# A gather row of 32 tokens by four expert slots in place of 128 tokens by one, and another order of the first gathers, sorts and projections

## The chip, the cores and the metric

The kernel runs on one core of a Trainium2 chip. The metric is device time in microseconds (us) of one execution: the median of three runs. The engines named are TensorE (PE), VectorE (DVE), ScalarE (ACT), GpSimd (POOL) and SyncE (SP). All arithmetic that matters here is float32.

## The reference

The input is 512 tokens of width 1024, with 16 learned "meta" tokens in front. There are two layers. The first has a mixer of attention and a short convolution, the second one of window means; both are followed by the same kind of expert layer, which makes nearly all of the time:

```python
def one_block(hb):                                   # tokens after rms_norm
    q = (hb @ w_query).reshape(t, 8, 2, 128)
    s = einsum('thpc,phkc->thpk', q, keys)           # 128 keys in each of two lists
    sv, si = lax.top_k(s, 16)                        # per list
    cand     = sv[:, :, 0, :, None] + sv[:, :, 1, None, :]
    cand_idx = si[:, :, 0, :, None] * 128 + si[:, :, 1, None, :]
    top_s, top_pos = lax.top_k(cand, 16)             # of 256 pairs
    idx  = take_along_axis(cand_idx, top_pos)        # (t, 8 heads x 16) experts
    gate = softmax(top_s)
    act  = gelu(einsum('tnd,td->tn', expert_u[idx], hb))
    return einsum('tn,tnd->td', gate * act, expert_v[idx])
h = h + one_block(rms_norm(h))
```

So each token has 128 slots: in each slot it fetches one of 16384 experts, a vector u for a dot with the token's `hb` and a vector v for a weighted sum. Kept together they are 8 KB.

## The kernel before

**Tiles and rows.** The 16 meta tokens are one job, the 512 others four tiles of 128 tokens, and there are two layers: after the meta tokens (they are needed in the first layer only) come the kernel's tiles 0 to 7, of which 0 to 3 are layer one. The unit of the stream is the *row*: one indirect gather of 128 partitions of 8 KB. For a tile, a row is one slot of all 128 tokens, so a tile has 128 rows; for the meta tokens, a row is 16 tokens by eight slots, so they have 16. In all there are 16 + 8 x 128 = 1040 rows. Sixteen rows are a *chunk*, four a *quad*.

**What a row does.** POOL issues the gather (line 1437) into a ring of six groups, each of 3 x 1024 floats a partition, so that u of one row lies over v of the row before. DVE multiplies u with `hb`, held in PSUM (`hd`), and sums along the width: a *dot* (line 1617). After each quad DVE starts the gelu (`gelu_argument`), ACT takes one exponential (line 1549), DVE makes four weights of it (`gelu_weights`, line 1599), and ACT writes, one row after the other, a matrix `w_col` with the weights on its diagonal (line 1559). PE multiplies it with v and adds into the open sum `y_ps` in PSUM: two matmuls of 128x512 a row (line 1496). For the meta rows `w_col` is 128x16, and four matmuls of 256 columns go to four groups of 32 PSUM partitions (line 1464). A gather into a ring group waits for the dot of the row before in that group and for the sum of the row before that (`Place`): with all six groups in use for the dot of row n-6 and the sum of row n-12.

**The order.** Each engine runs its own instructions in order; other engines are waited for by semaphores. The four functions of the last part write down that order by hand: `tile(j, hooks)` walks through the 128 rows of a tile, and a hook (row, step) puts another step behind that row. In this way the routing of the next-but-one tile (its queries on PE, eight steps of two matmuls each for one *piece* of two heads; the sort on DVE in thirteen stages, `topk_stages`) runs between the rows of tile j. Tiles 6 and 7 route nothing more.

**The beginning.** The mixer leaves `catT`, which PE multiplies with the output matrix: the *out-projection* (`project_tensor`, a half of 512 columns each call, numbered 2 to 9; 2 and 3 are tile 0, 4 to 9 tiles 1 to 3). Half 4 and later ones are taken to SBUF by ACT (`take_projected`). Two of the six ring groups, `ring_late`, lie where operands of these projections are, so they can be used only when all are done. The first eight gathers therefore go to the four early groups, and then POOL waits in `late_constants` for the last projection, before it clears `prev` and goes on:

```python
META_ORDER = [0, 1, 2, 3, 0, 1, 2, 3, 4, 5, 0, 1, 2, 3, 4, 5]
            gather_pool(pool, None, 0, range(EARLY_ROWS))          # eight
            late_constants(pool)
            gather_pool(pool, None, 0, range(EARLY_ROWS, CHUNK))
```

The meta tokens are routed first, all eight heads in one sort; PE then picks the 128 indices for each row out of the result with small matmuls (`meta_select_tensor`, line 1129), ACT stages them, and the first gather goes. Tile 0's first two pieces are queried and sorted in that time too (`first_query`), its other two between rows.

## Time and profile before

| what | value |
|---|---|
| median of 3 runs | 3069.64 us (3068.76 to 3072.61) |
| the profiled execution: its own time | 3071.45 us |
| its span, first to last instruction | 3069.7 us |
| first gather issued at | 337.81 us |
| PE busy | 85% of the span (line 1496: 4096 records, 1986 us) |
| DVE busy | 68% |
| POOL busy | 32% |
| ACT busy | 19% |
| mean granted clock of PE | 0.943 of full speed |
| moved by DMA | 1139 MB, 371 GB/s over the span |

How to read the rows: a time line starts with when it begins and how long it took, then engine, line of the kernel, operation, what it writes `<-` what it reads, shapes (partitions x elements), and how many instructions were put together in it; behind it, in brackets, is how long the engine stood idle before, and what it then waited for. A float32 matmul stands in these rows as two records, so "x16" is eight matmuls. `PEclk` is the clock that PE was granted, as a share of full speed. Lines of a window give for each engine its busy time and its instructions, then that clock, the share of time that the DMA engines were busy, and GB/s. Times of the rows count from the first instruction of the span.

### The profile page before, as it was taken

To read this page: it belongs to the slowest core of one execution; us is meant where nothing else is said; L and a number is where in the kernel's file an instruction comes from. 1 tells how busy PE (TensorE), PEld (TensorE's weight loads), DVE (VectorE), ACT (ScalarE), POOL (GpSimd) and SP (SyncE) were. 2 spreads that over 40 slices of the span, in tenths; PEclk is the share of its full clock that TensorE was granted. 3 is DMA by queue.
4 is the path that set the end of the run, shared out by engine and by line. 5 is a ranking of instruction groups with operands and counts; after the bars stand their busy time and mean duration, and the time that the engine had idled before them with its cause. 6 is when DMAs were issued, how large, how long until landed. Compare 5 with 4: busy or idle time off the path is not lost.

```text
span 3069.7 us, 27540 instructions
## 1 busy us (share of the span) xinstructions
PE 2618.8 (85%) x7006; PEld 1210.0 (39%) x7006; DVE 2096.7 (68%) x6440; ACT 582.0 (19%) x1769; POOL 997.0 (32%) x1107
## 2 busy tenths in 40 slices
PE   9999869897988789778988889888988889877777
PEld 4765424343443334333434334343434334333323
DVE  2143568887778668666788677866877688755555
ACT  2035112111111111112111211121112111111111
POOL 0000033333443333333333333333333333333332
PEclk9999989999999999889999999999998999999899
DMA  5131289999999999999999999999999999999998
GB/s 190 60 130 55 110 330 413 391 395 421 421 421 410 403 421 413 421 414 416 415 408 418 414 407 419 410 414 421 404 410 414 412 416 409 415 408 422 421 421 331
DMA packets 165560, 1139.24 MB, mean 371 GB/s; under 512 B 18672, under 2 KB 19696, under 8 KB 29984
## 3 DMA queue, kind: packets, MB, share of 16 engines
q0 software_dynamic: 149760, 1090.59, 86.6%
q1 hardware_dynamic: 15648, 46.94, 4.0%
q8 instruction: 57, 0.93, 0.1%
q14 instruction: 95, 0.78, 0.1%
HBM read 1135.30 MB, written 2.10 MB: 371 GB/s over the span
## 4 chain that ended last, share of the span: by engine, by line
DMA 50%; PE 33%; DVE 11%; issue 6%; ACT 1%; POOLq 0%; POOL 0%; SPq 0%; DVEq 0%
DMA ring_early<-in_peer_uv,idx_u 17%; DMA ring_early<-in_peer_vu,idx_u 17%; PE psum L1496 16%; DMA ring_late<-in_peer_uv,idx_u 9%; DMA ring_late<-in_peer_vu,idx_u 6%; PE psum L1071 5%; DVE ring_early L1617 4%; PE psum L713 3%; PE psum L755 2%; PE psum L616 2%; DVE ring_late L1617 2%; PE psum L649 1%; DVE work L1188 1%; DVE si L1186 1%; PE psum L578 1%
## 5 line engine op out<-in xcount | busy, mean ns | idle before, releaser
L1496 PE MATMUL psum<-ring_early,w_col 128*128 128x512 f32 x2736 | 1321.4, 626 | 252.3 <-ACT w_col L1559 238.8
L1617 DVE SCALAR_TENSOR_TENSOR ring_early<-ring_early,psum 128x1024 f32<-128x1024 f32 x696 | 846.9, 1217 | 413.5 <-DMA ring_early<-in_peer_uv,idx_u 209.7
L1496 PEld LDWEIGHTS psum<-ring_early,w_col 128*128 128x128 f32 x2736 | 537.3, 201 | 955.5 <-issue 789.5
L1496 PE MATMUL psum<-ring_late,w_col 128*128 128x512 f32 x1360 | 664.9, 628 | 123.3 <-ACT w_col L1559 113.6
L1617 DVE SCALAR_TENSOR_TENSOR ring_late<-ring_late,psum 128x1024 f32<-128x1024 f32 x344 | 418.6, 1217 | 222.9 <-DMA ring_late<-in_peer_uv,idx_u 144.7
L1437 POOL DMA_INDIRECT ring_early<-in_peer_vu,idx_u x348 | 329.2, 946 | 598.2 <-DVE ring_early L1617 285.9
L1437 POOL DMA_INDIRECT ring_early<-in_peer_uv,idx_u x348 | 326.8, 939 | 585.3 <-DVE ring_early L1617 307.7
L1559 ACT ACTIVATE w_col<-ident,weight 128x128 f32<-128x128 f32 x1024 | 343.9, 392 | 644.9 <-DVE weight L1599 638.3
L1496 PEld LDWEIGHTS psum<-ring_late,w_col 128*128 128x128 f32 x1360 | 267.3, 201 | 471.5 <-issue 407.9
L1549 ACT ACTIVATE ge<-ga 128x4 f32<-128x4 f32 (+1 forms) x265 | 54.3, 205 | 1359.7 <-DVE ga L1585 1359.7
L1071 PE MATMUL psum<-wq,hbT 128*128 128x512 f32 x512 | 274.5, 623 | 23.9 <-DVE work L1188 22.8
L1437 POOL DMA_INDIRECT ring_late<-in_peer_uv,idx_u x172 | 162.2, 943 | 293.9 <-DVE ring_late L1617 175.6
L1437 POOL DMA_INDIRECT ring_late<-in_peer_vu,idx_u x172 | 161.6, 940 | 269.5 <-PE psum L1496 116.5
L1071 PEld LDWEIGHTS psum<-wq,hbT 128*128 128x128 f32 x512 | 101.8, 201 | 157.6 <-issue 129.7
L505 POOL IOTA iota<- 128x16 f32 x1 | 0.1, 144 | 283.6 <-ACT catT L848 283.6
L713 PE MATMUL psum<-hT,w_ring 128*128 128x264 f32 x384 | 86.2, 387 | 1.7 <-ACT qkv L799 1.7
L713 PEld LDWEIGHTS psum<-hT,w_ring 128*128 128x128 f32 x384 | 72.7, 190 | 15.1 <-ACT qkv L799 2.0
L1593 DVE TENSOR_SCALAR ge<-ge 128x4 f32<-128x4 f32 (+1 forms) x265 | 44.2, 167 | 23.9 <-ACT ge L1549 23.9
L755 PE MATMUL psum<-w_ring,catT 128*128 128x512 f32 x128 | 57.2, 601 | 0.0
L1617 DVE DVE_READ_ACCUMULATOR ring_early<-ring_early,psum 128x1 f32 x696 | 57.1, 82 | 0.0
L616 PE MATMUL psum<-w_ring,hT 128*128 128x512 f32 x128 | 55.5, 594 | 0.0
L1595 DVE RECIPROCAL ge<-ge 128x4 f32<-128x4 f32 (+1 forms) x265 | 47.0, 177 | 9.1
(237 smaller groups left out, 1728.9 us busy)
## 6 DMA issues: line engine op xcount, KB each, us to landing
wq<-in_peer_w_query SPq DMA_DIRECT2D x16, 1024.0 KB, 18.0
w_ring<-in_even_w_in SPq DMA_DIRECT2D x5, 2048.0 KB, 8.1
ring_early<-in_peer_vu,idx_u POOLq DMA_INDIRECT x348, 12.9
ring_early<-in_peer_uv,idx_u POOLq DMA_INDIRECT x348, 12.9
w_ring<-in_even_w_out SPq DMA_DIRECT2D x1, 4096.0 KB, 13.9
ring_late<-in_peer_vu,idx_u POOLq DMA_INDIRECT x172, 12.9
ring_late<-in_peer_uv,idx_u POOLq DMA_INDIRECT x172, 12.9
hT<-in_x_T SPq DMA_DIRECT2D x4, 528.0 KB, 7.4
```

What stands on the lines that cost most here:

```text
L578: last = nc.tensor.matmul(psum[:, 4 + t, :], hT[:, k, block_of(t)], w_ring[:, 0, k, :], start=(k == 0), stop=(k == KD - 1))
L616: last = nc.tensor.matmul(psum[0:n, 4 + i % 4, :], hT[:, k, block_of(t)], w_ring[:, g % 2, k, :], start=(k == 0), stop=(k == KD - 1))
L713: last = nc.tensor.matmul(psum[:, 4 + 2 * (i % 2) + half, 0:HALF], w, hT[:, k, HALF * half:HALF * half + HALF], start=(k == 0), stop=(k == ...
L755: last = nc.tensor.matmul(dst, catT[:, k, cols_of(t)], w_out_sb[:, k, c], start=(i < 4 and k == 0), stop=(k == KD - 1))
L1071: ins = nc.tensor.matmul(dst[0:n, :], hbT[:, k, 0:n], wq[:, k, bass.ts(s, 512)], start=(k == 0), stop=(k == KD - 1))
L1437: nc.gpsimd.indirect_dma_start(pair_cells(at), None, uv_rows if at.side else vu_rows, bass.IndirectOffsetOnAxis(idx_u[par][:, i:i + 1], 0) ...
L1496: ins = nc.tensor.matmul(y_ps[:, half, :], w_col[:, i % W_SLOTS, :], v_cell(at)[:, 512 * half:512 * half + 512], start=False, stop=stop, s ...
L1549: nc.scalar.activation(ge[:, 0:n], ga[:, 0:n], ACT.Exp, scale=-GELU_B).then_inc(s_gexp, 1)
L1559: nc.scalar.activation(w_col[:, i % W_SLOTS, 0:cols], base[:, 0:cols], ACT.Copy, scale=weight[par][:, i:i + 1]).then_inc(s_wcol, 1)
L1593: c.did(nc.vector.tensor_scalar(ge[:, 0:n], ge[:, 0:n], 1.0, None, ALU.add))
L1595: c.did(nc.vector.reciprocal(ge[:, 0:n], ge[:, 0:n]))
L1617: nc.vector.scalar_tensor_tensor(out=cell, in0=cell, scalar=1.0, in1=rows, op0=ALU.mult, op1=ALU.mult, accum_out=dot[par][:, i:i + 1]).the ...
```

## The change

There are four parts.

1. *Four-slot layout.* A row of a tile is now 32 tokens (a *block*) by four slots. Eight rows of one block follow each other (a *run*, `RUN` = 8), then eight of the next block. DVE's dot needs the block's 32 rows of `hb` four times over, in the four groups of 32 partitions; eight matmuls of 32x512 make that for each run (`fill_tensor`), in the half of `hd` not in use, 12 rows ahead. That takes the place of ACT's one copy of `hb` a tile (`keep_scalar`). `w_col` is 128x32 (the weights on four 32x32 diagonals, `block_fold`), and the sum of a row is four matmuls of 32x256 to the four groups of 32 PSUM partitions, as for the meta rows. The indices and the gates of each chunk are put into the new arrangement by ACT: `stage_u` and `stage_gates`, eight copies of 32x8 each, in place of one copy of 128x16. The sum of a tile is opened by block (`open_block`, four matmuls) and taken by ACT in 16 copies of 32x256 (`take_blocks`) in place of two of 128x512. At the very end DVE makes half of the last eight copies, and the last tile is stored by rows 0 to 63 and 64 to 127 in place of by column halves. `hb` rotates over three buffers (`hb_of`).
2. *The first gathers.* `ORDER` puts the first 28 rows (16 meta, 12 of tile 0) on the four early groups, and `late_constants` comes behind them. With four groups, a gather waits for the dot of row n-4 and the sum of row n-8.
3. *The first sorts.* The first two sorts of tile 0 now both lie between the dots of the meta rows: the first with two stages behind each row from row 0, the second from row 8 on with one. `META_QUERIED` and `FIRST_QUERIED` (the row at which the last step of a query stands) move with them.
4. *Out-projection.* Half 3 goes behind the meta tokens' key scores. The norm of tile 0 on DVE goes into the meta sort. Half 4 goes behind both picks; halves 5 to 8 are cut into nine steps each (`project_step`), four steps behind each of the first meta rows' sums, half 9 two steps a row from row 10. ACT takes half 5 behind the column of row 3, and halves 6, 7 and 8 behind those of rows 5, 7 and 8.

The core of the diff:

```diff
+EARLY_TILE_ROWS = 12
+EARLY_ROWS = CHUNK + EARLY_TILE_ROWS
+ORDER = ([n % GROUPS_EARLY for n in range(EARLY_ROWS)] +
+         [(GROUPS_EARLY + n) % RING for n in range(2 * XT * TILE_ROWS - EARLY_TILE_ROWS)])
...
+        def project_step(pe, n):
+
+            i, k = 5 + n // PRODUCT_STEPS, n % PRODUCT_STEPS - 1
+            t, half = PROJECTED[i // 2], i % 2
+            c = slice(512 * half, 512 * half + 512)
+            if k < 0:
+                pe.wait_ge(s_mix, max(i - 3, 2))
+                nc.tensor.matmul(late_bank(i), ident[:, :], hres[:, t, c], start=True, stop=False)
+                return
+            ins = nc.tensor.matmul(late_bank(i), catT[:, k, cols_of(t)], w_out_sb[:, k, c], start=False, stop=(k == KD - 1))
+            if k == KD - 1:
+                ins.then_inc(s_proj, 1)
...
+        def fill_tensor(pe, f):
+
+            job, b = f // RUNS + 1, f % BLOCKS
+            pe.wait_ge(s_hb, job + 1)
+            if f:
+                pe.wait_ge(s_dot, CHUNK + RUN * (f - 1))
+            else:
+                pe.wait_ge(s_mix, 2 * XT - 1)
+            for half in range(2):
+                c = slice(512 * half, 512 * half + 512)
+                for g in range(BLOCKS):
+                    nc.tensor.matmul(rows_for((f + 1) % 2)[BLOCK * g:BLOCK * g + BLOCK, c],
+                                     ident[:, BLOCK * b:BLOCK * b + BLOCK], hb_of(job)[:, c],
+                                     start=True, stop=True).then_inc(s_fill, 1)
...
+        def open_block(pe, j, b):
+
+            if j == 0:
+                pe.wait_ge(s_mtaken, PARTS)
+            else:
+                pe.wait_ge(s_yadd, TAKEN * (j - 1) + TAKEN // 2 * (b // 2 + 1))
+            for n in range(PARTS):
+                nc.tensor.matmul(block_part(b, n), ident[:, block_rows(b)], tile_of(j % XT)[:, part_cols(n)],
+                                 start=(b % 2 == 0), stop=False, skip_group_check=True)
...
+                for n in range(PARTS):
+                    nc.tensor.matmul(block_part(b, n), w_col[:, i % W_SLOTS, :], v_cell(at)[:, part_cols(n)],
+                                     start=False, stop=last, skip_group_check=True).then_inc(s_acc, 1)
                 at_token(hooks, i)
...
+        def take_blocks(eng, copy, j, pair, parts=range(PARTS)):
+
+            eng.wait_ge(s_acc, PARTS * (CHUNK + TILE_ROWS * j + TILE_ROWS - RUN * 2 * (1 - pair)))
+            for b in (2 * pair, 2 * pair + 1):
+                for n in parts:
+                    copy(hres[block_rows(b), j % XT, part_cols(n)], block_part(b, n)).then_inc(s_yadd, 1)
...
+        def staged_cells(u, table, staging):
+
+            c = (u - 1) % TILE_CHUNKS
+            col = P * ((u - 1) // TILE_CHUNKS % 2) + 2 * TOPK * (c // 2)
             for half in range(2):
...
+                b = 2 * (c % 2) + half
+                for g in range(BLOCKS):
+                    yield (staging[BLOCK * g:BLOCK * g + BLOCK, RUN * half:RUN * half + RUN],
+                           table[block_rows(b), col + RUN * g:col + RUN * g + RUN])
...
         def stage_u(act, u, par):
 
             wait(act, s_dot, CHUNK * (u - 1))
             apart(act)
-            nc.scalar.copy(idx_u[par][:, :], idxT[:, cols(u)]).then_inc(s_idx_u, 1)
-
-        def columns_scalar(act, j, c, base, hooks=()):
+            if u == 0:
+                nc.scalar.copy(idx_u[par][:, :], idxT[:, cols(u)]).then_inc(s_idx_u, 1)
+                return
+            for cell, entry in staged_cells(u, idxT, idx_u[par]):
+                nc.scalar.copy(cell, entry).then_inc(s_idx_u, 1)
...
+        def stage_gates(act, u, par):
+
+            j, c = (u - 1) // TILE_CHUNKS, (u - 1) % TILE_CHUNKS
+            if j == 0:
+                act.wait_ge(s_pstep, 3 * (c // 2 + 1))
+            else:
+                act.wait_ge(s_gtab, j)
+            if u > 2:
+                act.wait_ge(s_gmul, QUADS * (u - 1))
+            for cell, entry in staged_cells(u, gateT, gate_u[par]):
+                nc.scalar.copy(cell, entry).then_inc(s_gate_u, 1)
...
-        META_QUERIED = (7, 23)
-        FIRST_QUERIED = (31, 47, 63, 79)
+        META_QUERIED = (13, 29)
+        SECOND_SORT = 8
+        FIRST_QUERIED = (34, 49, 64, 79)
...
+            for i, stage in enumerate(topk_stages(dve, 0, 0, P, meta=True)):
+                if i == 7:
+                    add_projected(dve, 3)
+                if i == 10:
+                    norm_vector(dve, 1, P, tile_of(0), 0)
...
+            early = ([(i // 2, first[i]) for i in range(TOPK_STAGES)] + [(7, lambda: piece_indices(dve, 0))] +
+                     [(SECOND_SORT + i, second[i]) for i in range(TOPK_STAGES)] +
+                     [(SECOND_SORT + TOPK_STAGES, lambda: piece_indices(dve, 1))] +
+                     routing_vector(dve, 1, META_QUERIED, 2, piece_indices))
+            dots_vector(dve, None, 0, of_chunk(early, 0) + [(11, lambda: piece_gates(dve, 0))])
...
+                hooks = list(hooks) + [(RUN * g - FILL_AHEAD, lambda g=g: fill_tensor(pe, RUNS * j + g))
+                                       for g in range(2, RUNS + 2 if j < LAST else RUNS)]
...
+            products = [(n // 4, lambda n=n: project_step(pe, n)) for n in range(4 * PRODUCT_STEPS)]
+            last = [(10 + n // 2, lambda n=n: project_step(pe, 4 * PRODUCT_STEPS + n)) for n in range(PRODUCT_STEPS)]
+            meta_sums_tensor(pe, products + last + [(8, lambda: fill_tensor(pe, 0)),
+                                                    (CHUNK + RUN - FILL_AHEAD, lambda: fill_tensor(pe, 1))] + of_chunk(early, 0))
```

Now the places where instructions change their order. **First pair, DVE, from the add of tile 0's first half to the meta sort's end.** L763 and L797 add a projected half to the tile, L377 to L384 and L392 to L399 are the refinement of the norm, L1030 and L1064 write `hb` of tile 0, L1212 and L1263 begin a sort. Before:

```order
L763 TENSOR_TENSOR hres<-hres,psum 128x512 [waits x_loaded0,out_projected,hb_ready]
L763 TENSOR_TENSOR hres<-hres,psum 128x512 [waits x_loaded0,out_projected]
L377 TENSOR_SCALAR newton_a<-ss 128x1 [waits h_rstd_guessed]
L378 TENSOR_TENSOR newton_b<-rstd 128x1
L380 TENSOR_TENSOR newton_b<-newton_b,newton_a 128x1 [waits h_newton_step]
L382 TENSOR_SCALAR newton_b<-newton_b 128x1 [waits h_newton_step]
L384 TENSOR_TENSOR rstd<-rstd,newton_b 128x1 [waits h_newton_step]
L1030 SCALAR_TENSOR_TENSOR hb<-hres,rstd,ffn_g 128x1024 [waits hb_kept_for_dots,hb_transposed,h_newton_step,ffn_gain_loaded]
L1212 MAX sv<-psum 128x8 [waits key_scores_ready,hb_ready,meta_scores_ready]
L1212 MAX sv<-psum 128x8 x3
L1186 MAX_INDEX si<-sv,psum 128x8 [waits topk_step]
```
After:

```order
L1286 TENSOR_TENSOR cand<-ta,iota16 128x256 [waits topk_step]
L1286 TENSOR_TENSOR cand<-ta,iota16 128x256
L1286 TENSOR_TENSOR work<-tb,iota16 128x256 x2
L392 TENSOR_SCALAR newton_a<-ss 128x1 [waits h_rstd_guessed]
L393 TENSOR_TENSOR newton_b<-rstd 128x1
L395 TENSOR_TENSOR newton_b<-newton_b,newton_a 128x1 [waits h_newton_step]
L397 TENSOR_SCALAR newton_b<-newton_b 128x1 [waits h_newton_step]
L399 TENSOR_TENSOR rstd<-rstd,newton_b 128x1 [waits h_newton_step]
L1064 SCALAR_TENSOR_TENSOR hb<-hres,rstd,ffn_g 128x1024 [waits hb_kept_for_dots,hb_transposed,h_newton_step,ffn_gain_loaded]
L1294 TENSOR_TENSOR cand<-cand,sif 128x256 [waits key_numbers_as_floats,onehot_step,hb_ready]
```
The second add (L797) now stands eight rows higher up, ahead of the eighth stage of the meta sort, and the norm ahead of its eleventh (L1294), with three stages still to come; before, both stood ahead of the sort.

**Second pair, PE, from the meta tokens' key scores to the picking of their indices.** L1112 and L1163 are the meta scores, L755 and L774 the projection of a half, L1145 and L1196 repeat the meta `hb`, L1064 and L1115 transpose tile 0's `hb`, the next lines are the first query and its scores, L1129 and L1180 pick. Before:

```order
L1112 MATMUL psum<-keysT,q_T 32x128 x15
L1145 MATMUL psum<-ring_early,spread 128x512 [waits hb_kept_for_dots,expert_constants_step]
L1145 MATMUL psum<-ring_early,spread 128x512
L1064 MATMUL psum<-ident,hb 128x128 [waits hbT_copied,w_query_loaded,queryT_copied,keys_loaded,hb_ready]
L1064 MATMUL psum<-ident,hb 128x128 x7
L1071 MATMUL psum<-wq,hbT 128x512 [waits hbT_copied]
L1071 MATMUL psum<-wq,hbT 128x512 x7
L1084 MATMUL psum<-ident,q_sb 128x128 [waits query_copied]
L1084 MATMUL psum<-ident,q_sb 128x128 x3
L1153 MATMUL psum<-keysT,q_T 128x128 [waits queryT_copied,key_scores_read]
L1153 MATMUL psum<-keysT,q_T 128x128 x3
L1129 MATMUL psum<-top_i,sel 128x16 [waits two_heads_routed]
```
After:

```order
L774 MATMUL psum<-w_ring,catT 128x512 x8
L1196 MATMUL psum<-ring_early,spread 128x512 [waits hb_kept_for_dots,expert_constants_step]
L1196 MATMUL psum<-ring_early,spread 128x512
L1115 MATMUL psum<-ident,hb 128x128 [waits hbT_copied,w_query_loaded,queryT_copied,keys_loaded,hb_ready]
L1115 MATMUL psum<-ident,hb 128x128 x7
L1122 MATMUL psum<-wq,hbT 128x512 [waits hbT_copied]
L1122 MATMUL psum<-wq,hbT 128x512 x7
L1135 MATMUL psum<-ident,q_sb 128x128 [waits query_copied]
L1135 MATMUL psum<-ident,q_sb 128x128 x3
L1204 MATMUL psum<-keysT,q_T 128x128 [waits queryT_copied,key_scores_read]
L1204 MATMUL psum<-keysT,q_T 128x128 x3
L1180 MATMUL psum<-top_i,sel 128x16 [waits two_heads_routed]
```
Eight matmuls of the projection came in between the meta scores and the rest; the first query stands ahead of the picking in both.

**Third pair, DVE, the first dots.** L1617 and L1691 are dots, L1646 to L1652 start a quad's gelu, and all other lines are stages of sorts. Before, the first two dots stand behind the whole first sort:

```order
L1248 TENSOR_REDUCE ia<-cand 128x32 [waits onehot_step]
L1249 TENSOR_REDUCE ib<-work 128x32
L1253 SCALAR_TENSOR_TENSOR top_i<-ia,ib 128x32 [waits topk_step,meta_gates_selected]
L1271 TENSOR_SCALAR idxT<-top_i 128x32 [waits two_heads_routed]
L1276 TENSOR_TENSOR soft<-top_s 128x32 [waits meta_gates_selected]
L1617 SCALAR_TENSOR_TENSOR ring_early,dot0<-ring_early,psum 128x1024 [waits rows_landed0,meta_rows_repeated]
L1617 SCALAR_TENSOR_TENSOR ring_early,dot0<-ring_early,psum 128x1024 [waits rows_landed1]
L1212 MAX sv<-psum 128x8 [waits key_scores_ready]
L1212 MAX sv<-psum 128x8 x3
L1617 SCALAR_TENSOR_TENSOR ring_early,dot0<-ring_early,psum 128x1024 [waits rows_landed2]
```
After, the first sort starts behind dot 0:

```order
L1691 SCALAR_TENSOR_TENSOR ring_early,dot0<-ring_early,psum 128x1024 [waits rows_landed0,meta_rows_repeated]
L1263 MAX sv<-psum 128x8 [waits key_scores_ready]
L1263 MAX sv<-psum 128x8 x3
L1237 MAX_INDEX si<-sv,psum 128x8 [waits topk_step]
L1237 MAX_INDEX si<-sv,psum 128x8 x3
L1239 MATCH_REPLACE work<-sv,psum 128x128 x4
L1691 SCALAR_TENSOR_TENSOR ring_early,dot0<-ring_early,psum 128x1024 [waits rows_landed1,key_scores_read]
L1249 MAX sv<-work 128x8 [waits topk_step]
L1249 MAX sv<-work 128x8 x3
L1255 MAX_INDEX si<-sv,work 128x8 [waits topk_step]
L1255 MAX_INDEX si<-sv,work 128x8 x3
L1691 SCALAR_TENSOR_TENSOR ring_early,dot0<-ring_early,psum 128x1024 [waits rows_landed2]
```
What was ahead of the first dot is now between dots 0 and 7, two stages a gap.

On PE the projection steps (L786 opens a half, L788 is one step) stand behind the sums of the meta rows, where the query steps stood; ahead of the first sum no half is left but number 4. On POOL, 28 gathers (lines L1488, all to `ring_early`) stand ahead of the clearing of `prev` in place of eight.

## Rows read from the trace of the kernel before

**Rows 1.** The page's DMA queues: packets, MB, share of 16 engines

```profile
q0 software_dynamic: 149760, 1090.59, 86.6%
```

**Rows 2.** Windows: PE, PEld, DVE, ACT, POOL busy; clock, DMA share, GB/s

```profile
396.00:450.00 54.00, 31.14 (x174) 10.80 (x175) 43.36 (x146) 8.88 (x35) 20.68 (x22) 0.77 0.99 397
747.00:2725.00 1978.00, 1687.53 (x4007) 755.43 (x4006) 1474.91 (x4543) 356.97 (x1138) 731.08 (x793) 0.94 1.01 414
2765.00:3040.00 275.00, 212.05 (x444) 87.59 (x443) 163.70 (x423) 41.86 (x145) 102.61 (x110) 0.94 1.01 420
1560.00:1570.00 10.00, 10.00 (x25) 4.46 (x24) 9.13 (x31) 0.79 (x4) 3.76 (x4) 1.00 0.97 345
2710.00:2720.00 10.00, 7.10 (x16) 2.96 (x16) 5.91 (x15) 1.64 (x8) 3.80 (x5) 1.00 1.01 421
```

**Rows 3.** Timeline of PE, 293 to 337 us

```profile
294.53 14.00 PE L755 MATMUL psum<-w_ring,catT 128*128 128x512 f32 x32
...
309.54 7.07 PE L1099 MATMUL psum<-wq,hbT 128*32 128x512 f32 x64 [0.42 <-ACT hbT L1021]
...
321.65 1.09 PE L1064 MATMUL psum<-ident,hb 128*128 128x128 f32 x8
...
333.20 1.13 PE L1153 MATMUL psum<-keysT,q_T 128*128 128x128 f32 x8 [0.77 <-ACT q_T L1089]
...
335.77 0.62 PE L1129 MATMUL psum<-top_i,sel 128*128 128x16 f32 x4 [1.44 <-DVE top_i L1253]
```

**Rows 4.** Timelines of DVE and POOL, 311 to 358 us

```profile
312.06 0.15 DVE L377 TENSOR_SCALAR newton_a<-ss 128x1 f32<-128x1 f32 x1 [2.81 <-ACT rstd L1016]
...
313.00 1.28 DVE L1030 SCALAR_TENSOR_TENSOR hb<-hres,rstd,ffn_g 128x1024 f32<-128x1024 f32 x1
...
320.12 0.89 DVE L1212 MAX8 sv<-psum 128x8 f32<-128x128 f32 x4 [5.84 <-PE psum L1112]
...
337.04 0.88 DVE L1212 MAX8 sv<-psum 128x8 f32<-128x128 f32 x4
...
346.30 0.17 DVE L1138 COPY gateT<-psum 128x16 f32<-128x16 f32 x1 [3.81 <-PE psum L1129]
...
356.78 1.21 DVE L1617 SCALAR_TENSOR_TENSOR ring_early<-ring_early,psum 128x1024 f32<-128x1024 f32 x1
...
337.81 1.10 POOL L1437 DMA_INDIRECT ring_early<-in_peer_vu,idx_u  x1 [42.70 <-ACT idx_u L1536]
```

**Rows 5.** POOL and DVE after 396 us; last, POOL's group over 396:3057

```profile
396.76 0.94 POOL L1437 DMA_INDIRECT ring_late<-in_peer_vu,idx_u  x1 [0.15 <-issue]
...
454.04 0.94 POOL L1437 DMA_INDIRECT ring_early<-in_peer_uv,idx_u  x1 [8.50 <-PE psum L1496]
...
405.60 1.22 DVE L1617 SCALAR_TENSOR_TENSOR ring_late<-ring_late,psum 128x1024 f32<-128x1024 f32 x1 [0.48 <-DMA ring_late<-in_peer_vu,idx_u]
...
L1437 POOL DMA_INDIRECT ring_early<-in_peer_vu,idx_u x344 | 325.3, 946 | 554.6 <-DVE ring_early L1617 285.9 <-PE psum L1496 215.7 <-issue 41.8
```

**Rows 6.** Timeline of PE, 373 to 436 us

```profile
373.12 7.03 PE L755 MATMUL psum<-w_ring,catT 128*128 128x512 f32 x16
...
402.36 0.62 PE L1464 MATMUL psum<-ring_early,w_col 128*16 128x256 f32 x8
...
434.35 1.96 PE L1520 MATMUL psum<-hres,ident 128*128 128x512 f32 x4 [0.70 <-ACT hres L1482]
```

**Rows 7.** Timeline of DVE: the dots of rows 30 and 144

```profile
462.91 1.22 DVE L1617 SCALAR_TENSOR_TENSOR ring_early<-ring_early,psum 128x1024 f32<-128x1024 f32 x1 [0.25 <-DMA ring_early<-in_peer_uv,idx_u]
...
760.42 1.22 DVE L1617 SCALAR_TENSOR_TENSOR ring_early<-ring_early,psum 128x1024 f32<-128x1024 f32 x1 [0.73 <-DMA ring_early<-in_peer_vu,idx_u]
```

**Rows 8.** Timeline of the end: PE and ACT

```profile
3059.51 7.10 PE L1496 MATMUL psum<-ring_early,w_col 128*128 128x512 f32 x16 [1.29 <-ACT w_col L1559]
...
3062.90 0.40 ACT L1559 ACTIVATE w_col<-ident,weight 128x128 f32<-128x128 f32 x1 [0.61 <-DVE weight L1599]
...
3066.66 0.59 ACT L1530 COPY hres<-psum 128x512 f32<-128x512 f32 x1 [0.27 <-PE psum L1496]
```

## What the change will do to the time

> **What bounds the kernel now.** I read the page's queue totals first. The indirect gathers move 1090.59 MB in 86.6% of the span of all 16 DMA engines [rows 1]: 1040 gathers of 128 x 8 KB, 1.049 MB each. Then the windows [rows 2]: from 396 us to 3040 us the DMA share is 0.99 to 1.01 and 397 to 420 GB/s flow, so the kernel is a prelude, a stream of gathers at about 2.5 us each (1.049 MB / 420 GB/s = 2.497), and a tail. PE is busy 85% over 747:2725 and DVE 75%, but both stand beside a full DMA. An edit can move the end in four places only: when the stream starts, what it loses while it starts, the gap between 414 and 420 GB/s in the routed tiles, and the tail.
>
> Third, the timeline of the prelude [rows 3, 4]. PE projects both halves of tile 0 until 308.5 (14.00 us), then runs the meta chain; the meta sort begins at 320.12, its indices are picked out at 335.77, the first gather is issued at 337.81. Only eight gathers go before 396.76, where POOL has waited for the last projection; DMA is idle most of that time. Fourth, waits after 396: POOL stood 8.50 us at the gather of 454.04 for a sum on PE [rows 5].
>
> **The change, part by part.** I sum against the profiled execution: 3071.45 us, a span of 3069.7; the median of the three runs is 1.8 lower.
>
> *The first gather.* Removed ahead of the meta chain: the second half of tile 0's projection, half of 14.00, so the meta sort starts 7.0 us earlier, at 313.1. Added inside it, on DVE, are one add of half a tile and the norm of tile 0 (first pair of orders, on DVE). The norm took from 312.06 to 314.28, 2.2 us [rows 4]; it now stands after ten of thirteen stages. The meta sort took 15.6 (320.12 to 335.77); ten stages are some 12.6 of it, plus 0.7 for the add: the norm starts at 326.4 and tile 0's `hb` is ready at 328.6. On PE the first query of tile 0 is queued ahead of the picking of the meta indices (second pair of orders, on PE), as before; but before, `hb` had long been there (PE was at its transposes at 321.65) and the query's scores ended at 334.33, just ahead of 335.77. These 12.7 us now start at 328.7: scores end at 341.4, and `top_i`, ready at 332, waits. Picking to gather takes 2.0. First gather 343.4, against 337.81. PE stands idle from 321.7 to 328.7, which it did not before. In the windows the granted clock was 0.77 over 396:450, where PE was busy 31 of 54 us, and 0.94 where it was busy 85%, so I add 1: 344.5, seven us **later**. Bounds: +4 (adds hidden) and +11 (the query at half clock).
>
> The Trainium skill ("TensorE: Matmul & The Clock Gate", Part 1) says that the array falls from 2.4 to 1.2 GHz after an idle stretch and returns only after sustained work. It speaks against this edit, and the 0.77 agrees in kind; by its two levels the first query of 7.0 us would cost up to 7 more, which is the +11 bound once more and not a number the sum uses.
>
> *From the first gather to tile 0.* Gathers 0 to 27 now run on the four early ring groups and need no projection, so they flow while PE projects. A gather into an emptied ring lands after 8.8 us (396.76 to 405.60, [rows 5]), with other loads beside it; I take 8.0, so dot 0 is at 352.5. The weights of the first quad come after dot 4, and now eight stages of the first sort lie between dots 0 and 3 (third pair of orders): 5 dots of 1.25, some 10 of that sort's 15.9 (337.04 to 356.78 less 3.8 of waiting), 1.2 of gelu: 370. Only then does PE's queue reach the projection steps, since they stand behind the first sum. PE has nothing from 364 to 370. After that it must do, in one FIFO:
> - 45 steps of 0.88 (a half tile, eight matmuls, took 7.03 [rows 6]): 39.6
> - eight query steps of 0.88: 7.0
> - 16 rows of sums, 0.62 each when alone [rows 6], taken as 0.75 between other work: 12.0
> - two fills of eight 32-row matmuls; 32 such matmuls of 32x512, four side by side, took 7.07 [rows 3], so 0.88 for four and 1.77 for a fill: 3.5
> - 2 for a cold start.
>
> Together 64, so PE is through at 434 and opens tile 0 at 436.5, against 434.35 before [rows 6]. With four groups gather n waits for the sum of row n-8, so POOL follows PE: gather 23 goes at 435, gather 24 (its row's exponential is behind the meta take on ACT) at 439. Then the ring fills: row 30 lands at 439 + 8 + 6 x 2.5 = 462, plus 1 to 4 us for the pool weights (1.6 MB) that now load in just that stretch: 464.5. Before, the dot of row 30 (rows counted from the first gather, 0; tile 0 starts at 16) began at 462.91, waiting for its DMA [rows 7]. So the 50 us of idle DMA that the change opens are **not** harvested: PE's FIFO takes the place of POOL's wait. Net 1.5 us later. Bounds: 8 earlier (row 24 at 430, the steps hidden behind dots) and 15 later (half of the 45 steps at the lower clock).
>
> *The four-slot layout.* Per row it replaces four passes of 0.44 (1.77 us: 16 records for four rows in 7.10 [rows 8]) by column groups like the meta sums, 0.62 [rows 6], and adds a fill, 1.77 for eight rows. PE is relieved of about 0.9 us a row, of 2.5. On the DMA that is worth only what PE costs it now. Sizes: over 747:2725, 1978 x (1 - 414/420) = 28 us lost against tile 7, which routes nothing. To split it I cut 1440:2720 in 128 windows of 10 us (the last and a bad one in [rows 2]): 25.1 us are lost against 421.5 GB/s, 16.6 of them in the 50 windows in which PE was busy 10.0 of 10. So two thirds, 19 us, at most are PE's. DVE is over 8.5 in the worse half of those windows and its load stays: I take 13 (bounds 0 and 25). In tile 0, rows 30 to 143 landed from 462.91 to 760.42 [rows 7], 297.5 us against 114 x 2.497 = 284.7: 12.8 lost. There the queries come every 15 rows in place of 16 and PE still waits for DVE to read the scores before the next query, now 8 rows behind it instead of 7; I take 5 (bounds -3 and 10).
>
> *ACT's new copies* (8 small ones for indices and 8 for gates in each 16 rows, 16 of 32x256 a tile) lie in ACT's idle 80% [rows 2]; their cover is the 7.5 us between a quad's weights and its next exponential. Cost 0; if the cover were gone, a rival below. *DVE's waits* for a fill: queued 12 rows ahead, 30 us, PE lags by 4 to 8 rows: 0. *Buffers of hb* rotate in three: 0.
>
> *The tail.* Before, PE had a backlog: the last weights column was written at 3062.90 + 0.40, PE ended at 3066.6, the last copy at 3067.25 [rows 8]. Now PE does one row, 0.6, then four small copies of 0.4 on each of two engines: 3065.5. Gain 1.8 (bounds 0 and 3).
>
> **Sum:** -1.5 + 13 + 5 + 1.8 = 18.3 gained: 3053 for the profiled execution, 3051 for a median.
>
> **Rivals.**
> A. *PE was the whole of the shallow queue*: all 28 and 12.8 come back and the prelude gains 1: 44 less 2, 3029. For: the worst 10 us (345 GB/s) had PE at 10.00. Against: DVE was at 9.13 in it.
> B. *DVE alone sets the queue's depth*: the routed tiles keep their 414 GB/s, tile 0 gains 2, the tail 1.8: 3067. For: POOL waits more for DVE's dots (285.9 us in these rows) than for sums (215.7) [rows 5]. Against: windows with only DVE above 9 lost 2.3 us of the 25.
> C. *Slower, the prelude*: the chain first weights, ACT takes one projected half, then the next w_col, then PE, runs in lock step and at the lower clock; 61 us of PE work stretch by half, 30 us later at row 30. It decides once tile 0 opens on PE after 455 instead of 436: 3081. For: ACT's take of each half now stands between columns, and an exponential waits behind it. Against: by my rows each half is done before ACT asks, twice only by a few us.
> D. *Slower, ACT*: a batch of 8 copies (1.6 us) delays exponentials, so dots, in the 41% of rows under a sort: 64 chunks x 2 x 0.41 x 1.6 = 84, half of it showing = 42: 3093. Against: ACT's 80% idle.
> E. *The layout does nothing to the DMA and the matmuls of four groups run one after another* (1.77 a row again): 3070. Against: 0.62 for eight records.
>
> **How the numbers follow.** Forecast 0.52, its own range 3038 to 3064; A 0.11, B 0.17, C 0.10, D 0.06, E 0.04. About 0.2%, 6 us, is what a measurement of this kernel can tell from no change. Under 3063.5 lie nearly all of the forecast, A and a fifth of B: 0.65. Between 3063.5 and 3075.8: most of B, E, edges of the forecast and C: 0.19. Above: C, D: 0.16. Leaving out a tenth at each end: 3030 to 3077.
>
> **What would show it.** First gather at 343 to 347 and behind the first query on PE. PE idle before the first sum, then dense until 434, POOL waiting for sums. Tile 0's first gather under four groups at about 410, row 30 landing at 464. PE busy near 55% of the stream, its clock often low without effect. GB/s over the routed tiles 417 or more; if it stays 414, B. ACT waits on DVE's weight, never DVE on ACT's ge for long; if DVE idles there, C or D. The forecast is wrong if row 30 lands before 455 or after 475.

## The result and the profile after

The changed kernel takes 3078.10 us (median of 15 runs, 3073.80 to 3079.93), the kernel before 3069.88 us (15 runs, 3067.91 to 3074.45). The ratio is 1.0023, with a 95% interval of 1.0016 to 1.0030: slower by 8 us, where 3051 was forecast. The profiled execution took 3077.79 us, its span is 3075.8.

The page of the changed kernel, its first part (busy us, share of the span, instructions):

```profile
PE 1907.1 (62%) x13374; PEld 784.8 (26%) x13374; DVE 2096.8 (68%) x6444; ACT 725.6 (24%) x2829; POOL 995.2 (32%) x1112
```

PE does a quarter less than before (2618.8 us there), DVE the same, ACT 144 us more. None of that shows in the time. Windows of the changed kernel (the columns of [rows 2]):

```profile
396.00:450.00 54.00, 42.12 (x222) 14.85 (x222) 27.71 (x84) 11.85 (x46) 15.99 (x17) 0.92 0.77 282
752.00:2730.00 1978.00, 1159.52 (x8800) 432.62 (x8796) 1474.22 (x4543) 465.20 (x1936) 728.09 (x792) 0.75 1.01 414
2770.00:3045.00 275.00, 127.86 (x1128) 47.76 (x1120) 161.40 (x420) 53.55 (x243) 101.65 (x109) 0.67 1.01 416
```

The second row answers to the second of [rows 2]: over 1978 us again (shifted by the 5 us that this kernel is late) PE is at 1160 in place of 1688 us and the granted clock at 0.75 in place of 0.94, with the same 414 GB/s. In the first row DMA is busy 0.77 of a stretch in which it was full before.

The beginning, on PE, answers to [rows 3]:

```profile
293.39 7.13 PE L774 MATMUL psum<-w_ring,catT 128*128 128x512 f32 x16
...
311.74 7.13 PE L774 MATMUL psum<-w_ring,catT 128*128 128x512 f32 x16
...
327.19 1.97 PE L1115 MATMUL psum<-ident,hb 128*128 128x128 f32 x8 [6.41 <-DVE hb L1064]
330.32 9.78 PE L1122 MATMUL psum<-wq,hbT 128*128 128x512 f32 x16 [1.16 <-ACT hbT L1055]
...
342.27 1.13 PE L1204 MATMUL psum<-keysT,q_T 128*128 128x128 f32 x8 [0.77 <-ACT q_T L1140]
343.24 0.52 PE L1180 MATMUL psum<-top_i,sel 128*128 128x16 f32 x4
...
434.51 0.64 PE L1552 MATMUL psum<-hres,ident 128*32 128x256 f32 x8 [1.81 <-ACT hres L1543]
```

And on DVE, where `top_i` was ready and where it waited for its picking:

```profile
325.85 1.28 DVE L1064 SCALAR_TENSOR_TENSOR hb<-hres,rstd,ffn_g 128x1024 f32<-128x1024 f32 x1
...
329.95 0.19 DVE L1304 SCALAR_TENSOR_TENSOR top_i<-ia,ib 128x32 f32<-128x32 f32 x1
...
343.79 0.17 DVE L1185 TENSOR_SCALAR idxT<-psum 128x16 uint32<-128x16 f32 x1 [13.35 <-PE psum L1180]
```

The indices of the meta tokens lay ready from 330.1 and were picked at 343.2, behind the first query of tile 0. PE had waited 6.41 us for `hb`. The transposes behind that wait took 1.97 us in place of 1.09 ([rows 3]), and the query 9.78 us, where the half tile of the same eight matmuls took 7.13 above: the granted clock was 0.50, the lower of its two levels (1.2 in place of 2.4 GHz), over the transposes and from 330.3 to 335.0, the first half of the query. The Trainium skill ("TensorE: Matmul & The Clock Gate", Part 1) says that PE falls to that level when idle; the trace agrees in kind, with some 2.7 us lost on this query and 0.9 on its transposes.

POOL's gathers in the changed kernel: the first of all, two long waits in tile 0 (at its rows 17 and 34), and the first ones of tiles 1 and 7:

```profile
345.18 1.10 POOL L1488 DMA_INDIRECT ring_early<-in_peer_vu,idx_u  x1 [50.25 <-ACT idx_u L1593]
...
468.23 0.94 POOL L1488 DMA_INDIRECT ring_early<-in_peer_uv,idx_u  x1 [11.68 <-PE psum L1567]
...
512.69 0.94 POOL L1488 DMA_INDIRECT ring_early<-in_peer_vu,idx_u  x1 [8.86 <-PE psum L1567]
...
752.72 2.25 POOL L1488 DMA_INDIRECT ring_early<-in_peer_vu,idx_u  x1 [1.51 <-issue]
...
2730.01 0.94 POOL L1488 DMA_INDIRECT ring_early<-in_peer_vu,idx_u  x1 [1.52 <-issue]
```

In the kernel before, these first gathers of tiles 1 and 7 went here:

```profile
747.43 2.24 POOL L1437 DMA_INDIRECT ring_early<-in_peer_vu,idx_u  x1 [0.88 <-DVE ring_early L1617]
...
2724.72 0.94 POOL L1437 DMA_INDIRECT ring_early<-in_peer_vu,idx_u  x1 [1.51 <-issue]
```

Both pairs are 5.29 us apart, so all of the loss but one us is there when tile 1 begins. That the two distances agree to the hundredth is chance: at the starts of the tiles between they are 5.00 to 5.89. What PE waited for ahead of the two long waits of POOL:

```profile
464.27 2.08 PE L1122 MATMUL psum<-wq,hbT 128*128 128x512 f32 x2 [9.62 <-DVE work L1239]
...
508.87 1.94 PE L1115 MATMUL psum<-ident,hb_b 128*128 128x128 f32 x8 [7.40 <-DVE work L1239]
```

The first step of a query, and the transposes of tile 1's `hb`, overwrite the bank in which the scores of the piece before stand, and so wait until DVE's sort has read them (the semaphore `key_scores_read`, which line 1239 raises). PE stands, the sums of the next rows stand behind it, and the gathers that need those sums wait too.

Of the gathers' times in each trace comes this table, on which most of what follows rests: microseconds a row, from a tile's first gather to the next one's, over 128 (tile 7 over 127). Tile 2, not shown, takes 2.72 in every kernel: the second layer's weights, 10 MB, load in it. Tile 5, not shown either, takes 2.549 to 2.557. Each row is one trace; where two kernels have the same order in tile 0 (changed and e5), they differ there by 0.007, 0.9 us in all.

| kernel | first gather | tile 0 starts | tile 0 | tile 1 | tile 3 | tile 4 | tile 6 | tile 7 |
|---|---|---|---|---|---|---|---|---|
| before | 337.81 | 413.30 | 2.610 | 2.541 | 2.542 | 2.534 | 2.550 | 2.528 |
| changed | 345.18 | 407.14 | 2.700 | 2.541 | 2.542 | 2.539 | 2.552 | 2.535 |
| e1, layout alone | 337.55 | 410.79 | 2.561 | 2.547 | 2.538 | 2.541 | 2.547 | 2.533 |
| e13, one step a row earlier | 336.77 | 411.95 | 2.586 | 2.546 | 2.538 | 2.542 | 2.548 | 2.534 |
| e8, 15 rows apart | 336.42 | 411.26 | 2.605 | 2.538 | 2.539 | 2.538 | 2.548 | 2.533 |
| e3, steps in pairs | 344.98 | 405.03 | 2.622 | 2.547 | 2.540 | 2.540 | 2.551 | 2.534 |
| e5, half dots | 346.35 | 408.44 | 2.693 | 2.543 | 2.542 | 2.540 | 2.549 | 2.535 |
| e6, pairs and picking | 332.40 | 400.36 | 2.619 | 2.546 | 2.541 | 2.540 | 2.550 | 2.535 |

### The profile page after: what moved, and what is told of

The parts are those of the page before. It is cut to its first block, busy times and chain, and to the rows that moved or that the text cites. A ratio compares the mean times of both kernels' runs of the same rounds, so it can differ in the third digit from the quotient of the medians.

```text
span 3075.8 us, 41833 instructions
## 1 busy us (share of the span) xinstructions
PE 1907.1 (62%) x13374; PEld 784.8 (26%) x13374; DVE 2096.8 (68%) x6444; ACT 725.6 (24%) x2829; POOL 995.2 (32%) x1112
## 4 chain that ended last, share of the span: by engine, by line
DMA 58%; PE 20%; DVE 10%; issue 10%; ACT 1%; POOL 0%; POOLq 0%; DVEq 0%; SPq 0%; ACTq 0%
DMA ring_early<-in_peer_uv,idx_u 22%; DMA ring_early<-in_peer_vu,idx_u 20%; DMA ring_late<-in_peer_vu,idx_u 8%; DMA ring_late<-in_peer_uv,idx_u 8%; PE psum L1567 3%; PE psum L1122 3%; PE psum L732 3%; DVE ring_early L1691 2%; PE psum L635 2%; PE psum L1100 2%; PE psum L668 1%; PE psum L788 1%; DVE work L1239 1%; PE psum L597 1%; DVE si L1237 1%
## 5 line engine op out<-in xcount | busy, mean ns | idle before, releaser
L1691 DVE SCALAR_TENSOR_TENSOR ring_early<-ring_early,psum 128x1024 f32<-128x1024 f32 x702 | 854.7, 1217 | 452.6 <-DMA ring_early<-in_peer_vu,idx_u 238.7
L1567 PE MATMUL psum<-ring_early,w_col 128*32 128x256 f32 x5488 | 535.3, 496 | 729.8 <-ACT w_col L1626 672.1
L1691 DVE SCALAR_TENSOR_TENSOR ring_late<-ring_late,psum 128x1024 f32<-128x1024 f32 x338 | 411.5, 1218 | 215.3 <-DMA ring_late<-in_peer_uv,idx_u 137.2
L1488 POOL DMA_INDIRECT ring_early<-in_peer_vu,idx_u x352 | 331.7, 942 | 638.7 <-DVE ring_early L1691 352.3
L1488 POOL DMA_INDIRECT ring_early<-in_peer_uv,idx_u x350 | 328.4, 938 | 578.8 <-DVE ring_early L1691 369.2
L1567 PE MATMUL psum<-ring_late,w_col 128*32 128x256 f32 x2704 | 267.2, 492 | 335.2 <-ACT w_col L1626 305.8
L1567 PEld LDWEIGHTS psum<-ring_early,w_col 128*32 128x32 f32 x5488 | 190.4, 133 | 1108.0 <-issue 768.4
L1626 ACT ACTIVATE w_col<-block_fold,weight 128x32 f32<-128x32 f32 x1024 | 268.7, 313 | 657.7 <-DVE weight L1668 642.9
L1488 POOL DMA_INDIRECT ring_late<-in_peer_uv,idx_u x168 | 157.7, 938 | 306.7 <-DVE ring_late L1691 239.3
L1488 POOL DMA_INDIRECT ring_late<-in_peer_vu,idx_u x170 | 159.6, 939 | 247.6 <-DVE ring_late L1691 110.8
L1567 PEld LDWEIGHTS psum<-ring_late,w_col 128*32 128x32 f32 x2704 | 94.2, 132 | 515.3 <-issue 381.9
L1100 PE MATMUL psum<-hb_b,ident 128*32 128x512 f32 x768 | 144.4, 886 | 0.0
L1100 PE MATMUL psum<-hb,ident 128*32 128x512 f32 x768 | 140.3, 863 | 0.8 <-ACT hres L803 0.8
L1596 ACT COPY idx_u<-idxT 32x8 uint32<-32x8 uint32 x512 | 99.1, 194 | 11.7
L1608 ACT COPY gate_u<-gateT 32x8 f32<-32x8 f32 x512 | 99.1, 194 | 11.7
L1100 PE MATMUL psum<-hres,ident 128*32 128x512 f32 x512 | 98.2, 904 | 0.0
```

The lines of the kernel that those rows point to most:

```text
L1100: nc.tensor.matmul(rows_for((f + 1) % 2)[BLOCK * g:BLOCK * g + BLOCK, c], ident[:, BLOCK * b:BLOCK * b + BLOCK], hb_of(job)[:, c], start=T ...
L1488: nc.gpsimd.indirect_dma_start(pair_cells(at), None, uv_rows if at.side else vu_rows, bass.IndirectOffsetOnAxis(idx_u[par][:, i:i + 1], 0) ...
L1567: nc.tensor.matmul(block_part(b, n), w_col[:, i % W_SLOTS, :], v_cell(at)[:, part_cols(n)], start=False, stop=last, skip_group_check=True) ...
L1596: nc.scalar.copy(cell, entry).then_inc(s_idx_u, 1)
L1608: nc.scalar.copy(cell, entry).then_inc(s_gate_u, 1)
L1626: nc.scalar.activation(w_col[:, i % W_SLOTS, 0:base.shape[-1]], base[:, :], ACT.Copy, scale=weight[par][:, i:i + 1]).then_inc(s_wcol, 1)
```

## The experiments

Ratios are to the kernel before, run beside each; its median lay between 3070.1 and 3071.3 us in them. A difference of 1 us between two medians of this table is not told from none.

| label | median us | ratio, 95% interval |
|---|---|---|
| e1_layout | 3064.29 | 0.9983 (0.9974 to 0.9992) |
| e3_rows | 3065.91 | 0.9984 (0.9975 to 0.9993) |
| e4_pick | 3073.12 | 1.0010 (1.0001 to 1.0019) |
| e5_half_dots | 3076.26 | 1.0018 (1.0009 to 1.0027) |
| e6_rows_pick | 3060.61 | 0.9968 (0.9956 to 0.9980) |
| e7_layout_pairs | 3064.16 | 0.9977 (0.9968 to 0.9986) |
| e8_layout_15 | 3069.80 | 1.0000 (0.9991 to 1.0009) |
| e9_pairs_only | 3066.91 | 0.9984 (0.9975 to 0.9993) |
| e10_tail | 3060.76 | 0.9968 (0.9956 to 0.9980) |
| e11_light0 | 3061.16 | 0.9967 (0.9955 to 0.9979) |
| e13_step_early | 3068.03 | 0.9992 (0.9983 to 1.0001) |

**The layout alone (e1).** Parts 2 to 4 of the change are taken back:

```diff
-ORDER = ([n % GROUPS_EARLY for n in range(EARLY_ROWS)] +
-         [(GROUPS_EARLY + n) % RING for n in range(2 * XT * TILE_ROWS - EARLY_TILE_ROWS)])
+ORDER = META_ORDER + [n % RING for n in range(2 * XT * TILE_ROWS)]
...
-        META_QUERIED = (13, 29)
-        FIRST_QUERIED = (34, 49, 64, 79)
+        META_QUERIED = (7, 23)
+        FIRST_QUERIED = (31, 47, 63, 79)
```

> The four-slot layout alone, with the order of before: ring order, clearing of prev after eight gathers, sorts, projections and query rows as before. Theory (the layout neither helps nor hurts, the new order costs): median within 2 us of before, 3069 to 3072; tiles 1 to 6 take 2.54 us a row as in both kernels. Rival (the layout itself costs, by ACT's many small copies or by PE's lower clock): 3075 to 3079, as the changed kernel, with the loss inside tile 0. Rival of the prediction (layout gains in routed tiles, and the order ate it): 3057.

None of the three: it gains 6 us. The layout is good for the time and the new order costs 13.8 (3064.29 to 3078.10). The gain is in tile 0, 2.561 us a row in place of 2.610, which is 6.3 us over 128 rows. (Its trace also starts tile 0 2.5 us earlier than before, where e7 and e13, with the same beginning, start it 1.2 and 1.4 earlier.) The layout gives the routed tiles nothing, with PE relieved as in the changed kernel.

Where tile 0 gains is seen at the waits behind queries, seven rows ahead of what they wait for in both kernels (how these rows are counted stands below). POOL waited 8.75, 9.51 and 9.35 us behind them in the kernel before, at rows 53, 69 and 85, and waits 7.49, 7.58 and 7.49 here. The first of these in the kernel before; its counterpart of e1 is shown below:

```profile
556.84 0.94 POOL L1437 DMA_INDIRECT ring_late<-in_peer_vu,idx_u  x1 [8.75 <-PE psum L1496]
```

That it is PE's lighter load that shortens them, and no other part of the layout, is argued and not shown.

**PE's waits in tile 0 (e3, e9).** The query steps between rows of tile 0 (and of the meta rows before it) go two behind a row in place of one (`a_row` = 2), so that a query's first step stands three rows ahead of its last, not seven. In e3 the transposes of tile 1's `hb` move from row 21 to 26 too (and ACT's copies of them from 24 to 28), in e9 they stay:

```diff
-                hooks += [(at + 1 - KD + k, query(p, s, k)) for k in range(KD)]
+                hooks += [(at - (KD - 1 - k) // a_row, query(p, s, k)) for k in range(KD)]
...
-            tile(0, [(at - CHUNK, f) for at, f in early if at >= CHUNK] + [(21, lambda: start_tensor(pe, 2, P, 0))] +
-                 routing_tensor(pe, 2, FIRST_QUERIED) + start_stages_tensor(pe, 3, None, FIRST_START))
+            tile(0, [(at - CHUNK, f) for at, f in early if at >= CHUNK] + [(26, lambda: start_tensor(pe, 2, P, 0))] +
+                 routing_tensor(pe, 2, FIRST_QUERIED, 0, 2) + start_stages_tensor(pe, 3, None, FIRST_START))
```

> The changed kernel; in tile 0 PE's query steps go two behind a row in place of one, so a query's first step stands four rows later, and the transposes of tile 1's hb stand at row 26 in place of 21. Theory (tile 0 lost 4 us because PE, now close behind DVE, stands in its queue at steps that wait for scores which DVE reads nine rows later, and the sums behind them hold gathers back): the two stalls of POOL for PE at rows 17 and 34 of tile 0 (11.7 and 8.9 us) fall under 4 us, tile 1's first gather comes 3 to 6 us earlier than 752.7, median 3072 to 3075. Rival (DVE or the DMA is what lost, PE's stall only shows it): no change, 3078.

The mechanism holds and is at work five times, not two: 12.2 us gained, where 3 to 6 were expected (POOL's other long waits of the changed kernel, 9.3, 9.4 and 10.9 us at rows 55, 70 and 85, go as well). The gathers that stood at 468.23 and 512.69 stand here:

```profile
456.04 0.94 POOL L1488 DMA_INDIRECT ring_early<-in_peer_uv,idx_u  x1 [0.71 <-issue]
...
500.53 0.94 POOL L1488 DMA_INDIRECT ring_early<-in_peer_vu,idx_u  x1 [0.79 <-DVE ring_early L1691]
```

> The changed kernel with tile 0's query steps two behind a row, but the transposes left at row 21, nine rows ahead of the reading they wait for. Together with the moved transposes it took 12.2 us off. Theory (five waits, each with its share): the stall of 8.9 us at row 34 stays and costs 2 to 4, 3068 to 3070. Rival (one of the waits carried it all): 3066 or 3078.

The wait at row 34 stays (8.80 us), and e9 is 1.0 us above e3, less than the 2 to 4 expected: nearly all of the 12 hangs on the queries' steps. These two medians alone do not tell 1 us from nothing; in the traces e9's dots fall 1.7 us further behind e3's at that wait (rows 20 to 36).

**The picking ahead of the first query (e4), and both (e6).**

```diff
             meta_rows_tensor(pe)
+            pe.wait_ge(s_routed, 2)
+            meta_select_tensor(pe, top_i, META_IDX, s_midx)
             start_tensor(pe, 1, P, 0)
+            pe.wait_ge(s_idx, 1)
...
-            pe.wait_ge(s_routed, 2)
-            meta_select_tensor(pe, top_i, META_IDX, s_midx)
```

ACT stages the indices ahead of its copies for that query, and DVE takes the meta gates behind dot 0.

> The changed kernel with the picking of the meta indices ahead of tile 0's transposes and first query on PE. First gather at 335 in place of 345. Theory (from the first gather to tile 0 all hangs on PE's queue, about 64 us of work after the first two queries): row 30's dot comes 2 to 5 us earlier than 464.3, median 3074 to 3076. Rival A (the first gather is worth its whole 10 us): 3068. Rival B (PE's first query now ends later and the gain is nil): 3078 or more.

The first gather goes at 332.56, 12.6 us earlier, and 5.0 us of it arrive in the median, one us more than the range expected; the dot of row 30 comes 4.8 earlier. The rest is lost before row 30, where by the theory PE's queue takes it.

> Both edits of the two runs before on the changed kernel: query steps of tile 0 two behind a row with the transposes at row 26 (it alone took 12.2 us off the median), and the picking ahead of the first query (it alone took 5.0 off). Theory (two separate places, PE's queue before row 16 and PE's waits in tile 0): the gains add, 3060 to 3062. Rival (with PE's waits gone, tile 0 hangs on DVE, which works off the first two sorts between dots; what comes earlier is waited for there): 3064 to 3066.

The gains add (17.5 us off the changed kernel, 12.2 and 5.0 alone). This version beats both kernels: 9 to 10 us under the one before, and 3.7 under e1, which has the layout alone.

**What sets a row at 2.54 us (e5, e11).** Half of each dot is left out on DVE, in tiles 1 to 7 (e5, on the changed kernel) or in tile 0 (e11, on e6):

```diff
-                nc.vector.scalar_tensor_tensor(out=cell, in0=cell, scalar=1.0, in1=rows,
+                w = D if j is None or j == 0 else D // 2
+                nc.vector.scalar_tensor_tensor(out=cell[:, 0:w], in0=cell[:, 0:w], scalar=1.0, in1=rows[:, 0:w],
...
```

> The changed kernel with DVE's dots from tile 1 on over 512 of the 1024 columns: that leaves out half of each of these dots and takes some 0.5 us a row off DVE, gathers unchanged in number and size. Theory DVE (its sorts set the queue's depth and so the 2.54 us a row): tiles 1 to 6 fall to 2.50 to 2.52 us a row, 15 to 25 us faster than the changed kernel, 3053 to 3063. Rival DMA (the transfers themselves take 2.54): under 3 us faster. The prediction's split (two thirds PE, one third DVE) would give at most 9 us here.

The window over tiles 1 to 6 of e5:

```profile
752.00:2730.00 1978.00, 1157.88 (x8788) 430.39 (x8784) 1079.93 (x4545) 465.36 (x1937) 730.18 (x792) 0.75 1.01 415
```

DVE is at 1080 us in place of 1474, and 415 GB/s flow in place of 414. It is the rival, DMA: with PE a third lighter, and then DVE a quarter lighter, the gathers take the same time, and the DMA engines are busy 1.01 of it. POOL's issuing (0.94 us a gather, 37% of this window) and ACT were not varied; both are far from full.

> The kernel of both edits with DVE's dots of tile 0 alone over 512 of the 1024 columns (half of each of these dots is left out), some 0.5 us a row off DVE. Tile 0 takes 2.619 us a row there, the tiles after it 2.54 to 2.55. Theory (without PE's waits, tile 0 under the new order hangs on DVE, which has four sorts and two norms in 128 rows and starts them late): tile 0 at 2.55 to 2.58, 5 to 9 us faster, 3052 to 3056. Rival (DMA, filling the ring behind PE's queue in the first rows): under 2 us, 3059 to 3061.

Again the rival: tile 0 at 2.614 in place of 2.619, the median 0.5 us higher than e6. What tile 0 still loses there lies in its first rows. Windows of e6:

```profile
410.00:480.00 70.00, 48.98 (x315) 17.58 (x314) 47.59 (x157) 14.81 (x61) 24.53 (x26) 0.84 0.95 372
480.00:560.00 80.00, 52.99 (x378) 21.23 (x376) 70.26 (x246) 21.33 (x87) 29.35 (x31) 0.82 1.01 418
560.00:736.00 176.00, 106.34 (x794) 41.49 (x792) 151.66 (x497) 41.93 (x172) 65.54 (x70) 0.74 1.01 414
```

From 480 us on it flows at 414 to 418 GB/s; before that, 372. In the changed kernel the same three stretches have 330, 407 and 398 (the last to 740), at a DMA share of 0.86, 0.99 and 0.98.

**How many rows of waiting are free (e7, e8, e13).** On the layout alone: e7 puts the steps in pairs as e9 does. e8 takes the changed kernel's rows for tile 1's queries (first cut below), e13 moves one step of each of these queries one row ahead (second cut, with `ahead` = 1).

```diff
-        FIRST_QUERIED = (31, 47, 63, 79)
+        FIRST_QUERIED = (34, 49, 64, 79)
```

```diff
-                hooks += [(at + 1 - KD + k, query(p, s, k)) for k in range(KD)]
+                hooks += [(at + 1 - KD + k - (ahead if k == 0 else 0), query(p, s, k)) for k in range(KD)]
```

> The layout alone, in the order of before, with tile 0's query steps two behind a row. In the layout alone POOL stood 6.8, 7.5, 7.6 and 7.5 us at rows 13, 53, 69 and 85 of tile 0 behind such steps. Theory (in the layout alone these are nearly hidden by the gathers in the ring, tile 0 being at 2.561 us a row against 2.54 in the other tiles): those stalls go, gain 1 to 3 us, 3061 to 3063. Rival (a stall costs as in the changed kernel, some 3 us each): 3053.

No gain at all, under the 1 to 3 us expected: the waits go and nothing else does.

> The layout alone, in the order of before, but with the changed kernel's query rows of tile 1's routing, 34, 49, 64, 79 in place of 31, 47, 63, 79: 15 rows apart in place of 16, so that PE's first step of a query stands 9 rows ahead of DVE's reading of the scores that it waits for, in place of 8. Theory (the cost of the new order is in this spacing): 3 waits each one row of 2.5 us longer, of which little is hidden any more: 3069 to 3072. Rival (the spacing is harmless, the cost came from the first sorts now lying between dots): 3064.

> The layout alone, in the order of before (3064.3), 16 rows between queries as there, and one thing moved: the first of a query's eight steps of tile 1's routing stands one row earlier on PE, right behind the scores of the piece before, as with 15 rows between queries; DVE's order is that of the layout alone. Counted anew by the hooks, that first step stands 7 rows ahead of DVE's reading of those scores in the layout alone, and 8 here and with 15 rows between (the two expectations on these waits said 8 and 9, one too many). Theory (it is PE's wait that costs, and it shows once it is longer than 7 rows): three waits of 8 rows, 3068 to 3071, as with 15 rows between (3069.8). Rival (what cost there was the sorts' place on DVE, moved to later and closer rows): 3064 to 3065.

With queries 15 rows apart the layout loses 5.5 us, and with that one step moved, DVE's order untouched, 3.7. The rows count as follows: a query's last step stands at row q, its scores at q+8, DVE reads them at q+16. The next query's first step stands at q+9 with 16 rows between, seven rows ahead of what it waits for, and at q+8 with 15 rows, or in e13: eight. (The expectations of e3, e8 and e9 count one row too many.) The wait of POOL in the middle of tile 0 (its row 53, then row 52), in e1 and in e13:

```profile
552.91 0.94 POOL L1488 DMA_INDIRECT ring_late<-in_peer_vu,idx_u  x1 [7.49 <-DVE ring_early L1691]
```

```profile
553.58 0.94 POOL L1488 DMA_INDIRECT ring_late<-in_peer_vu,idx_u  x1 [9.98 <-PE psum L1567]
```

Of 2.5 us more of waiting, three times, 3.7 us arrive in the median; of the 6.8 to 7.6 us that POOL waits four times in e1, nothing did (e7). In e1 all three gathers go on with a dot that was the last to come, in e13 two of three with a sum. What e8 loses beyond e13 (1.8 us) is not separated: its queries also stand later and closer together. With 14 rows between queries this order deadlocks, so no run shows what a ninth row costs.

**The tail (e10).** The last 64 rows of e6 are stored as two column halves, each behind its own engine's copies:

```diff
...
-                sp_.wait_ge(s_yadd, TAKEN * LAST + TAKEN // 2 * (pair + 1))
-                sp_.dma_start(out[0, P * (XT - 1) + n * pair:P * (XT - 1) + n * pair + n, :],
...
+            sp_.wait_ge(s_yadd, TAKEN * LAST + TAKEN // 2 + TAKEN // 4)
+            sp_.dma_start(out[0, at + n:at + P, 0:512], hres[n:P, XT - 1, 0:512]).then_inc(s_out, 16)
+            sp_.wait_ge(s_right, TAKEN // 4)
+            sp_.dma_start(out[0, at + n:at + P, 512:1024], hres[n:P, XT - 1, 512:1024]).then_inc(s_out, 16)
```

> The kernel of both edits (3060.6 us), with the last 64 rows stored as two column halves, each as soon as its engine has copied it, in place of one store behind both. Theory (of the tail's missing 1.8 us some 0.8 went into a store of 64 x 4 KB behind both engines' copies, where before 128 x 2 KB went, and 1 into the copies): from the last copy to the end of the span 0.3 to 0.8 us less, the median 3059.8 to 3060.4, which the medians will hardly tell apart. Rival (the store's time is fixed, whatever its size): no change or, with one more store to issue, up to 0.5 more.

From the start of ACT's last copy to the end of the span it is 4.8 us (3053.89 to 3058.7), in e6 5.1 (3053.71 to 3058.8); the medians are the same. By these two traces a third of a us at most lies in the store's form, a little under the theory's 0.3 to 0.8.

## Why the prediction was wrong

**The first gather** was put at 344.5 and stood at 345.18, behind the first query, as forecast. That the two are so close is in part luck: the part for the lower clock was taken as 1 us and was some 3.6 (query and transposes), and `hb` came 1.5 us earlier than worked out.

**From there to row 30** the forecast was 1.5 us later than before. The dot of row 30 stands here:

```profile
464.25 1.22 DVE L1691 SCALAR_TENSOR_TENSOR ring_early<-ring_early,psum 128x1024 f32<-128x1024 f32 x1
```

That is 1.3 later than in [rows 7]. PE opened tile 0 at 434.5 (436.5 forecast), and PE's queue took the place of POOL's wait: the first of the windows above shows DMA at 0.77 while PE works. This part holds, and rival C, which needed tile 0 to open after 455, fell.

**Tile 0**, from row 30 to tile 1, was to gain 5 us and lost 4.3 (the dot of row 144 is 5.6 later, 1.3 of it from before row 30). Here the step "PE still waits for DVE to read the scores before the next query, now 8 rows behind it instead of 7; I take 5" failed. The gain that it counted on exists: the layout alone takes rows 30 to 143 in 291.5 us in place of 297.5. Where it went is seen in how late a dot comes against the same dot of the kernel before (us; rows of tile 0; negative is earlier):

| kernel | row 16 | row 20 | row 52 | row 68 | row 92 | row 128 |
|---|---|---|---|---|---|---|
| changed | 0.1 | 4.6 | 5.4 | 5.4 | 5.2 | 5.6 |
| e9, steps in pairs | -0.1 | 0.6 | 2.3 | -0.1 | -5.5 | -4.5 |
| e1, layout alone | -2.3 | -1.6 | -2.4 | -4.2 | -9.0 | -8.0 |
| e13, one step a row earlier | -1.4 | -1.4 | -1.7 | -2.0 | -4.2 | -3.5 |

Two kinds of wait did it. The first is one that the step does not name: the query whose first step stands at row 6 of tile 0, seven rows ahead of DVE's reading, behind which POOL stood 11.68 us. Between rows 16 and 20 the changed kernel falls 4.5 us behind, and e9, which has the same times up to row 16 and its first step four rows later, falls 0.7. Seven rows cost nothing in e1 (e7), but there a gather waits for the sum of row n-12, and here that of row 17 waits for the sum of row 7, n-10, since `ORDER` gives rows 14 to 17 of tile 0 to the four early groups, whose last two uses then lie 6 and 10 rows back. That this is why seven rows are too many here is read from the code; no run moved this wait by itself. The second are the three waits of eight rows. From row 52 to row 92 the layout alone gains 6.6 us on the kernel before, the changed kernel 0.2, and e13, with e1's order but for the one step, 2.5. So in the changed kernel the eight-row waits took back nearly all that the layout gives there, where the step had put them at a part of it. The count of rows was right, and its price was not.

**The routed tiles** were to gain 13 us (28 lost, two thirds PE's) and gained 0.0: 5.29 us behind at tile 1, 5.29 at tile 7. Two steps failed. One is the 28: "1978 x (1 - 414/420)". The 420 is a window of 275 us that leaves out the first 16 gathers of tile 7, which took 2.64 us each. A window over all of that tile reads 417, which by the same formula is 14 us:

```profile
2724.00:3045.00 321.00, 248.76 (x519) 102.54 (x518) 189.46 (x492) 49.87 (x171) 119.01 (x127) 0.94 1.01 417
```

Counted by gathers alone, tile 7 takes 2.528 us each (1.0486 MB / 2.528 us = 414.8 GB/s) and tiles 1 and 3 to 6 take 2.534 to 2.556, 2.545 in the mean: 11 us in 640 rows. The other step is that two thirds of the loss are PE's. They came from the 50 windows of 10 us in which PE was at 10.00 of 10, though in 28 of them 410 GB/s or more flowed, and against 421.5 GB/s, a pace of windows four gathers long. e1 and the changed kernel take that PE load away, e5 takes DVE's too, and the mean of the same five tiles stays at 2.545 us in the changed kernel and in e5. What the remaining difference to tile 7 hangs on is open. Rival B was right on the routed tiles and its reason, DVE, was wrong: it is DMA. Rival A fell (its 3029 is 42 us under the profiled execution; for a median, as the other rivals have it, that is 3028).

**ACT's copies** cost nothing that shows, as forecast (e1 has them all), and so rival D fell; rival E fell by tile 0's gain in e1 and by the 0.64 us of a row's four matmuls (last section).

**The tail** was to gain 1.8 and gained 0.1: from the last dot's start to the end of the span 9.4 us after, 9.5 before. PE's backlog is gone as forecast. Here are the last steps:

```profile
3069.06 0.32 ACT L1626 ACTIVATE w_col<-block_fold,weight 128x32 f32<-128x32 f32 x1 [0.61 <-DVE weight L1668]
...
3070.73 1.51 ACT L1576 COPY hres<-psum 32x256 f32<-32x256 f32 x4 [1.34 <-PE psum L1567]
...
3070.73 1.80 DVE L1576 COPY hres<-psum 32x256 f32<-32x256 f32 x4 [1.70 <-PE psum L1567]
```

From the written column to the start of the copies it is 1.35 us, where [rows 8] has 3.36 (3063.30 to 3066.66): 2.0 gained. The copies take 1.80 in place of 0.59 (1.2 lost), and from their end to the span's end it is 3.3 in place of 2.45 (0.8 lost). The copies were in the forecast as 1.6; the 0.8 was not, since the forecast stopped at the last copy. The other kernels with this tail take 9.4 us or 8.9, as their last sum runs at the lower level of PE's clock (1.08 us, as here) or at the higher (0.64 us, in e6, e11 and e13), so half a us of it is chance. Tile 7 itself lost another 0.9 us (from 5.29 to 6.16 at the last dot), as in all kernels with the layout (2.533 us a row or more, 2.528 before); no run explains it.

So the forecast failed in three terms: 13 us for a gap that PE's load did not make, 9 between the gain and the loss of tile 0's waits, and 1.7 for the copies and the store of the tail. With tile 7's 0.9 they make up the way from 18.3 gained to 6.3 lost in the profiled executions to within 0.2.

## What to carry to other kernels

Before pricing a gain against "full bandwidth", take that bandwidth from a whole repeated unit (bytes over the time from one tile's first transfer to the next one's), and test whether a lighter load makes the unit any faster: a window over part of a unit read 0.7% high here, half of the gap that was to be won. A wait in an in-order queue has an amount that the buffers hide and an edge behind it: count, in rows, how far ahead of its releaser a waiting step stands and how far back the buffers reach at that place, and when an order is rewritten keep both where they were. Here one row more cost 1 to 2 us each time, with all work the same, and one wait of the old length at a place where the buffers reach back less cost some 4. In the changed kernel, issuing the waiting steps more densely and later was worth 12 us, and in e1, where the buffers already hid them, nothing.

## What the runs showed of the hardware

A row's four matmuls of 32 weight columns by 256, to the four groups of 32 PSUM partitions, took 0.64 us where the granted clock was 1.00 and 1.08 where it was 0.50. Two rows of the changed kernel:

```profile
471.14 0.64 PE L1567 MATMUL psum<-ring_early,w_col 128*32 128x256 f32 x8
...
3069.53 1.08 PE L1567 MATMUL psum<-ring_early,w_col 128*32 128x256 f32 x8 [1.51 <-ACT w_col L1626]
```

The last sum of e6 took 0.64, behind the same wait of 1.5 us for its column.

PE's granted clock averaged 0.75 over tiles 1 to 6 in place of 0.94, and the gathers came no later for it. An ACT copy of 32x8 took 0.19 us (194 ns, the mean of 512), one of 32x256 0.38 (1.51 for four) and one of 128x512 0.59: a copy of 256 elements pays a third of the price of one of 65536. And the gathers held 2.54 us a row, 413 GB/s, under PE loads from 1160 to 1688 us and DVE loads from 1080 to 1475 in the same 1978 us.
